# First norm's root applied at the evacuations, keys and values between the two query groups, HGRN sigmoids one panel later

## The reference

```python
def rmsnorm(x, g):
    y = x * lax.rsqrt(jnp.mean(x * x, axis=-1, keepdims=True) + EPS)
    return y * g

u = rmsnorm(h, norm_mix_g)
p = jnp.einsum('bsd,de->bse', u, w_in) + b_in
aq, ak, av, hq, hf, hi, hg, gate_a, gate_b = split_columns(p)
y_attn = sliding_window_sink_attention(aq, ak, av, attn_sinks)
y_hgrn = hgrn2_branch(hq, hf, hi, hg, lb, hgrn_norm_g)
#   in hgrn2_branch:
#   log_f = log(lb + (1 - lb) * sigmoid(hf));  k = (1 - lb) * sigmoid(-hf);  q = silu(hq)
```

## Time and profile before

| | us |
|---|---|
| median of 3 runs | 791.05 (790.82 to 792.37) |
| the profiled execution | 790.83 |
| its span | 789.1 |

### The profile page before, as it was taken

How to read it: one execution, slowest core, us unless ns; L and a number is a source line. 1 busy time by engine, 2 the same in 40 slices (tenths; PEclk the granted TensorE clock), 3 DMA queues, 4 the chain that set the end, 5 groups by cost and what they waited for, 6 DMA issues and landing times. The chain is left out here.

```text
span 789.1 us, 12516 instructions
## 1 busy us (share of the span) xinstructions
PE 777.0 (98%) x5048; PEld 687.0 (87%) x5048; DVE 607.1 (77%) x815; ACT 476.1 (60%) x727; POOL 18.6 (2%) x38
## 2 busy tenths in 40 slices
PE   8999999999999999999999999999999999999996
PEld 8978978898888898888888888999789999999885
DVE  5587788687887667887869897997878788777464
ACT  6855887568644384444334267876858667665451
POOL 3000002000200000000000000001000000000000
PEclk9999999999999999999999999999999999999999
DMA  8873644656546638799879993644363756555611
GB/s 302 296 261 127 227 138 149 208 186 215 174 161 213 214 107 283 269 305 315 276 242 339 336 380 126 222 135 133 108 213 111 237 175 200 167 172 170 240 53 54
DMA packets 106537, 162.54 MB, mean 206 GB/s; under 512 B 4576, under 2 KB 51824, under 8 KB 106480
## 3 DMA queue, kind: packets, MB, share of 16 engines
q1 hardware_dynamic: 106336, 161.48, 61.3%
q10 hardware_dynamic: 144, 0.26, 0.1%
HBM read 160.67 MB, written 1.06 MB: 205 GB/s over the span
## 5 line engine op out<-in xcount | busy, mean ns | idle before, releaser
L1175 DVE TENSOR_TENSOR wL<-raw,wH 128x2048 fp32r<-128x2048 f32 (+2 forms) x142 | 285.2, 2013 | 84.3 <-ACT wH L764 81.9
L764 ACT ACTIVATE wH<-raw 128x2048 fp32r<-128x2048 f32 (+1 forms) x114 | 212.1, 1864 | 91.7 <-PE ps L1866 61.1
L1863 PE MATMUL ps<-p1H,wH 128*128 128x256 f32 x784 | 224.0, 286 | 1.6 <-DVE arena L1175 0.8
L1863 PE MATMUL ps<-p1H,wL 128*128 128x256 f32 x784 | 221.2, 283 | 0.0
L1863 PE MATMUL ps<-p1L,wH 128*128 128x256 f32 x784 | 219.8, 283 | 0.0
L1863 PEld LDWEIGHTS ps<-p1H,wH 128*128 128x128 f32 x784 | 150.2, 192 | 5.5 <-DVE wL L1175 2.2
L1863 PEld LDWEIGHTS ps<-p1H,wL 128*128 128x128 f32 x784 | 150.2, 192 | 0.0
L1863 PEld LDWEIGHTS ps<-p1L,wH 128*128 128x128 f32 x784 | 149.5, 192 | 0.0
L1866 PE MATMUL ps<-wH,p1H 128*128 128x512 f32 x316 | 125.2, 396 | 0.0
L1866 PE MATMUL ps<-wL,p1H 128*128 128x512 f32 x316 | 123.2, 390 | 0.0
L1866 PE MATMUL ps<-wH,p1L 128*128 128x512 f32 x316 | 123.1, 390 | 0.0
(11 more groups left out here) (303 smaller groups left out, 946.3 us busy)
## 6 DMA issues: line engine op xcount, KB each, us to landing
raw<-in_w_in SPq DMA_DIRECT2D x37, 1024.0 KB, 6.1
raw<-in_w_ada SPq DMA_DIRECT2D x24, 1024.0 KB, 5.2
raw<-in_w_up SPq DMA_DIRECT2D x44, 512.0 KB, 4.7
raw<-in_w_ffn_gate SPq DMA_DIRECT2D x22, 512.0 KB, 4.3
raw<-in_w_ffn_up SPq DMA_DIRECT2D x22, 512.0 KB, 5.5
raw<-in_w_ffn_down SPq DMA_DIRECT2D x10, 1024.0 KB, 5.5
raw<-in_w_down SPq DMA_DIRECT2D x10, 1024.0 KB, 5.1
raw<-in_w_out SPq DMA_DIRECT2D x8, 1024.0 KB, 5.1
```

The source lines that it names most:

```text
L764: nc.scalar.activation(wH[:, q % NHL, 0:nk, 0:wd], raw[:, i % NRAW, 0:nk, 0:wd], ACT.Copy).then_inc(on.w_hi, 1)
L1175: return v.tensor_tensor(o, a, b, op)
L1863: last = mm(ps[:, t[1], 0:T], wt[:, slot, k, t[2]:t[2] + P], at_[:, k0 + k, :], start=st, stop=en)
```

## The change

Four things are altered, all in the first block.

- **Root.** The first norm no longer multiplies by 1/rms. x comes in four channel quarters (256 KB each, all tokens), each followed by one row block of the first weight panel. TensorE transposes one quarter (`turn_input`) ahead of the products and one behind each of the first three steps; ScalarE writes `p1H` straight from PSUM with the gain as scale, VectorE `p1L`. Squares and roots (`root_0`) follow behind the first panel, the spread behind the first tile of kv. 1/rms is multiplied in where products are evacuated: VectorE evacuates q, kv, hq, hf (`ROOTED`) with `rbs0`, and ScalarE then adds the bias in place; the token-major groups take it as a scalar of each token. `rbs0` lies in the memory of `dtW`, so `dtW` is filled in the first FFN.
- **Order.** q0, kv, q1; q0's evacuation stands behind kv's first panel event, `vectors` there too, `setup` behind q1's first panel. V is turned into bank 7, and the first `pt` waits for its copy.
- **Sigmoids.** Those of hq and hf move from the evacuation to the tail, behind the next group's first panel event.
- **Banks.** Some groups use other PSUM banks.

The diff, cut to its core:

```diff
+    for _name, _c, _b, _f in (("q", 0, 0, 2), ("hq", 1280, 0, 2), ("hf", 2304, 4 * _i, 2 - 2 * _i)):
+        GROUPS[f"{_name}{_i}"] = group("w_in", [(_c + _i * W, W)], cm_tiles(_b, _f), "DDDD", "P1")
+    for _name, _c, _b in (("hi", 3328, 2 - 2 * _i), ("hg", 4352, 2 * _i), ("ga", 5376, 2 - 2 * _i), ("gb", 6400, 2 - 2 * _i)):
...
+GROUPS["kv"] = group("w_in", [(1024, 256)], [("cm", 4, 0), ("cm", 5, P)], "DD", "P1")
...
+ROOTED = ["kv"] + [f"{_n}{_i}" for _i in range(2) for _n in ("q", "hq", "hf")]
...
-                tl.append(("evac", name))
-                if name.rstrip("0123456789") in ("f", "u", "xs", "bc", "hf"):
+                (later if name == "q0" else tl).append(("evac", name))
+                if name.rstrip("0123456789") in ("f", "u", "xs", "bc", "hq", "hf"):
                     later.append(("tail", name))
...
-    gemm("q0")
-    gemm("q1", [("vectors",)], [("setup",)])
+    gemm("q0", [("root",)])
+    gemm("kv", [("vectors",)])
     first = X(0, "ga0", 0)
-    gemm("kv", [], first[:-1] + [("v_turn",)] + first[-1:])
+    gemm("q1", [("setup",)], first[:-1] + [("v_turn",)] + first[-1:])
...
-    gemm("hi1", [("hdm", 1), ("hprep", 1, 0)], [("hprep", 1, 1)])
+    gemm("hi1", [("hdm", 1)], [("hprep", 1, 0), ("hprep", 1, 1)])
...
+            x = IN["x"][0].rearrange("(j p) n -> p j n", p=P)
             for k in range(KP):
+                sp.dma_start(res[:, :, wide(k)], x[:, :, wide(k)]).then_inc(on.in_x[k], 16)
                 sp.dma_start(raw[:, 0, k, :], first[:, k, 0:W]).then_inc(on.in_w0[k], 16)
                 if k == 0:
+                    sp.dma_start(par[:, 0:KD], IN["params"][:, 0:KD]).then_inc(on.in_g, 16)
+            sp.dma_start(par[:, KD:], IN["params"][:, KD:]).then_inc(on.in_par, 16)
```

ScalarE: the start, then the evacuation of q and the tail of hf:

```diff
+            def enter():
+
+                table(ACT.Sqrt)
+                act.wait_ge(on.in_g, 16)
+                for k in range(KD):
+                    if k % 2 == 0:
+                        act.wait_ge(on.ut_psum, k // 2 + 1)
+                    nc.scalar.activation(p1H[:, k], xT(k), ACT.Copy, scale=gain(0, k)).then_inc(on.uh_done, 1)
+                    if k < 4:
+                        first_hi(0, k, 1)
+                    elif k in (4, 5):
+                        first_hi(1, 2 * k - 8, 2)
+
+            def root_0():
+
+                for j in range(TB):
+                    square_x(j)
+                    root(0, j)
...
+                    if i == 0:
+                        act.wait_ge(on.in_par, 16)
+                        act.wait_ge(on.rb_psum, 1)
+                        nc.scalar.activation(rbs0, rb, ACT.Copy).then_inc(on.rb_copy, 1)
+                    for m in range(4):
+                        act.wait_ge(*EV[name, m])
+                        nc.scalar.activation(aQ[:, 4 * i + m], aQ[:, 4 * i + m], ACT.Identity,
+                                             bias=pc("b_in", 4 * i + m)).then_inc(on.evac_act, 1)
...
+                elif g == "hf":
+                    for m in range(4):
+                        act.wait_ge(*EV[name, m])
+                        nc.scalar.activation(T2[:, m], T1[:, m], ACT.Sigmoid, scale=-1.0,
+                                             bias=negb[:, 4 * i + m:4 * i + m + 1])
+                        nc.scalar.activation(T1[:, m], T1[:, m], ACT.Sigmoid,
+                                             bias=pc("b_in", 18 + 4 * i + m)).then_inc(on.evac_act, 1)
```

VectorE's evacuations:

```diff
+                if name in ROOTED:
...
+                    if name == "q0":
+                        dve.wait_ge(on.in_par, 16)
+                        dve.wait_ge(on.rb_copy, 1)
...
+                    for m, t in enumerate(GROUPS[name]["tiles"]):
+                        dve.wait_ge(on.tile_done, TILE[name, m])
+                        tt(to[m], ps[:, t[1], 0:T], rbs0, ALU.mult).then_inc(on.evac_dve, 1)
...
-                        tt(to, ps[:, GROUPS[name]["tiles"][j][1], :], rows(name)[0], ALU.add).then_inc(on.evac_dve, 1)
+                        stt(to, ps[:, GROUPS[name]["tiles"][j][1], :], R1[:, j:j + 1], rows(name)[0], ALU.mult,
+                            ALU.add).then_inc(on.evac_dve, 1)
```

TensorE:

```diff
+            def turn_input(c):
+
+                pe.wait_ge(on.in_x[c], 16)
+                if c > 1:
+                    pe.wait_ge(on.u_ready, 2 * c - 2)
+                for k in (2 * c, 2 * c + 1):
+                    for j in range(TB):
+                        last = tr(xT(k)[:, j * P:(j + 1) * P], res[:, j, k * P:(k + 1) * P])
+                last.then_inc(on.ut_psum, 1)
...
+                        if q == 0 and k < 3:
+                            turn_input(k + 1)
...
+                        if (name, part, m) == ("kv", 0, 0):
+                            spread_roots(0)
...
+                    if n == 0:
+                        warm(2)
+                        turn_input(0)
+                        warm(4)
+                        continue
```

and in `pt` of group 0:

```diff
+                    else:
+                        pe.wait_ge(on.v_done, 1)
```

More of the change, by code:

```diff
@@ L790, in square_x @@
             def square_x(j):
-                act.wait_ge(on.in_x[j], 16)
+                for c in range(4):
+                    act.wait_ge(on.in_x[c], 16)
                 if j:
@@ L1049, in _ @@
                     norm(e[1])
+                elif k == "root":
+                    root_0()
                 elif k == "evac":
@@ L1249, in read_ada, with enter @@
                    f(pc("b_ada", c, 16)), ALU.add).then_inc(on.ada_done, 1)
+            def enter():
+                dve.wait_ge(on.in_g, 16)
+                for k in range(KD):
+                    if k < 4:
+                        first_lo(0, k, 1, k == 3)
+                    elif k in (4, 6):
+                        first_lo(1, k - 4, 2, k == 6)
+                    dve.wait_ge(on.uh_done, k + 1)
+                    stt(p1L[:, k], xT(k), gain(0, k), p1H[:, k].bitcast(F32), ALU.mult, ALU.subtract).then_inc(on.u_ready, 1)
             def norm(n):
                 if n == 0:
-                    turn_over(n, 0)
+                    enter()
+                    return
                 if n == 4:
@@ L1474, in tail @@
                     tt(zL[:, 2 * i:2 * i + 2], zps if i in TOKENS_FIRST else ZT, zH[:, 2 * i:2 * i + 2].bitcast(F32), ALU.subtract).then_inc(on.z_ready, 1)
+                    if i == 5:
+                        dve.wait_ge(on.in_dtw, 16)
+                        step(v.memset(dtW[:], 0.0))
+                        v.tensor_copy(dtW[:, :, 0:8], dtw).then_inc(on.dtw_lo, 1)
                 elif g == "u":
@@ L1789, in late_turn, with spread_roots @@
             def late_turn(n, k):
[L1791 removed]
+                pe.wait_ge(*((on.rb_copy, n + 1) if k == 6 else (on.tmp_done, 8 * (n - 1) + 2)))
                 turn(n, (k,), range(TB)).then_inc(on.ut_psum, 1)
+            def turn_input(c):
[6 more added lines that the diff above has]
+                last.then_inc(on.ut_psum, 1)
+            def spread_roots(n):
+                for j in range(TB):
+                    pe.wait_ge(on.rd_done, 2 * n + j + 1)
+                    last = spread(rb[:, j * P:(j + 1) * P], R1[:, j:j + 1])
+                last.then_inc(on.rb_psum, 1)
             def gate_sum(g, i):
@@ L1894, in panel @@
                         early = k == 0 and name in NORM_OF
-                        if early:
+                        if q == 0 and k == 0:
+                            pe.wait_ge(on.uh_done, 1)
+                            pe.wait_ge(on.first_hi, 1)
+                            for t in g["tiles"]:
+                                product(t, 0, only=(0,))
+                        elif early:
                             pe.wait_ge(on.uh_done, 8 * NORM_OF[name] + 1)
@@ L1907, in panel @@
                                 pe.wait_ge(on.gate_done, 2 if name == "f0" else 4)
-                            last = product(t, k, only=(0, 2) if early else (0, 1, 2))
+                            last = product(t, k, only=(2,) if early and q == 0 else (0, 2) if early else (0, 1, 2))
                         if early:
```

184 lines of the change are left out of this document (72 added, 112 removed).

## The result

The changed kernel takes 803.3 us in the median of four runs (801.88 to 803.79), the kernel before 790.93 in four runs on the same chip: a ratio of 1.0150 (95% interval 1.0138 to 1.0163), slower by 12.4 us. The forecast was 801.1, the range 795.2 to 803.9. The profiled execution took 801.88 and its span is 800.1, 11.0 us more than the 789.1 of before. The other three took 803.2 to 803.8; an execution of that kind was profiled later (last experiment).

The account below looks back on a forecast made before the run. TensorE was taken to set the time once it has work, so a later stall adds in full. The profiled 790.83 plus 6.6 and 3.7 gave 801.1 us, range 795.2 to 803.9.

Parts of the forecast that it names:

- First term: From the start to group 0's first transposes of probabilities: late q1 part 1 and the waits after it, +6.6 us, start included.
- The wait of 2.2 us for bank 2: At ga0's first product: TensorE waits 2.2 us until VectorE evacuates q1's first tile, which holds the bank.
- The start: At the first panel: first product at 6.7 rather than 9.42, worth 1.6 us at the end of q0.
- The stall of 0.4 for quarter 1: In q0's first part, ahead of step 2: preparing quarter 1 takes 2.2 us against 1.9 of TensorE work, stall 0.4.
- Second term: At the tail of hf0: its late sigmoids delay PT and the transposes of group 5, +3.7 us (2.4 to 4.8).
- The line between the two rows of weights: Landing of q1 part 0's weights, read between panel 3 (21.54) and panel 4 (26.17): 24.5; 22.5 was taken.
- The step that ends at 14.7: At the start: the last of q0's four product steps, forecast to end at 8.6, 10.5, 12.8 and 14.7.
- rival 6: At every table switch on ScalarE: a drain is paid besides the load, 806.6 us in all, chance 0.02.
- Edits at nothing: Other evacuations, hf1's sigmoids, dtW's fill and queue changes: costed at nothing, bounds together -0.3 and +0.7.
- Rival 1: At the first group and hf0's tail: both stalls hidden, the start kept, 789.2 us, chance 0.07.

Follow-up runs that it names:

- last experiment: The changed kernel itself, unaltered, profiled a third time to see one of its slower executions: 803.78 us.
- the order at the front: Changed kernel with VectorE evacuating q0 and kv before the next low part, biases added later, vectors and setup behind q1 part 0: 795.26 us, ratio 1.0054.
- the early evacuation alone: Kernel with hf0 early, with the vectors put back behind q0 while VectorE still evacuates q0 and kv early: 794.89 us.
- the kernel with hf0 early: Changed kernel with the order at the front, V turned earlier, hf0's sigmoids back in its evacuation, and VectorE evacuating hf0 before a low part: 790.61 us, ratio 0.9996.

## Why the prediction was right, and where it was not

**First term, predicted +6.6, measured +7.1** (transposes of group 4 at 114.66 against 107.59). The chain came as written: weights at 22.8 (22.5), evacuation of q0 from 27.0, vectors to 33.7 (33.3), high part, low part, start at 37.98 (37.5), stall 4.45 (4.45); V's copy at the end of that chain let TensorE go at 55.07 (54.65). The runs show the mechanism from three sides: taken away by the order at the front, lengthened by the vectors done twice, halved by the early evacuation alone. Behind the stall two errors cancelled. The wait of 2.2 us for bank 2 wasn't there, since q1 part 1 took 8.1 us rather than 5.9 at the lower clock; with TensorE kept busy, the wait appears as 2.14, and in the third profile, where the panel took 1.5 us more, as 0.65. VectorE's chain, which the prediction had right, set ga0's start each time. That the clock cost no more than this wait could take up was luck: nothing in the prediction bounded it.

**The start, predicted 1.6 at the end of q0, measured 1.2** (20.9 against 22.1), and not steady: q0 part 1 began anywhere from 14.78 to 16.36 in the profiles of kernels with the same start, where 16.3 was the row of before. In the changed kernel it doesn't matter: the chain runs from the landing of q1 part 0's weights. The first product came at 5.87, before the 6.7 of the prediction, for the second lot of warming began at 4.42 rather than 4.9 and took 1.45 us up to the first product rather than 1.8; with eight matmuls at the lower clock throughout it took 1.57 (4.46 to 6.03 in the kernel with hf0 early), so the clock had little part in it. The stall of 0.4 for quarter 1, ahead of step 2, wasn't there. Instead 1.00 us stood ahead of step 1, since the second weight row had not landed until 7.4, and 0.39 ahead of part 1. The step that failed is that I asked of no later weight row when it lands.

**Second term, predicted +3.7, measured +4.0** in the profiled execution (11.08 at the panel behind the transposes of group 5, less 7.07). Gaps 1.23 (1.05) and 2.03 + 0.28 (2.7); from start to start they cost 0.5 us more than their idle time. Eight sigmoids took 3.3 us (3.1), at 0.40 each.

**Slips in the prediction's working.** The line between the two rows of weights gives 24.7 us and not 24.5; 22.8 was measured, near the 22.5 taken. The step that ends at 14.7 holds a second wait of 0.4 us that is not named. In rival 6 the two terms should be 10.7 and 5.1 and not 10.3 and 5.5, with the same sum. None of them enters the forecast, since the chain starts from the 22.5 taken.

**What was missed: the clock behind a stall.** Where the clock falls behind the gap at group 5, the second term is 5.6 rather than 4.0; that is about what lies between the profiled 801.88 and the median of 803.3. The other 0.8, from 801.1 to 801.88, are the two terms (0.5 and 0.3). The prediction held a stall to cost its own length. The Trainium skill ("TensorE: Matmul & The Clock Gate", HAM oscillation — how this bites in real kernels) says that the lower clock comes back after an idle gap and that the work behind it pays. The trace agrees, with 0.51 for 5.2 us, and I had not priced it. Here a gap of 2 us cost 3.6 where no other wait took it up (vectors put back behind q0: 2.05 and 1.5).

**Edits at nothing, -0.3 to +0.7.** In the changed kernel nothing of them shows. But that was cover: with the sigmoids back in place hf0's two-step evacuation cost 1.1 to 1.2 us at TensorE, until it was made early. Rival 1, both stalls hidden, I had at 789.2; with both mended and hf0 early the kernel stands at 790.6. The start gives less than its 1.6, and 0.60 us at the first transposes is left. No version that was tried is measurably faster than the kernel before.

**Rival 6**, a drain of 1.4 us at each switch of tables: the Trainium skill ("ScalarE: Activation LUTs", What ACT_TABLE_LOAD costs) states it. Six loads in a row at 1.28 with 0.22 between them, and a stall that grew by 4.51 us for three more, rule it out here.

## What to carry to other kernels

When one evacuation is split over two in-order queues, ask of the first step what stands ahead of it there: each time VectorE's product stood behind a weight's low part, ScalarE stood still and everything queued on it came later. Count the stall behind the stall (here a bank) before hoping for a gain from moving one wait: with the vectors moved 4.4 us went and 5.4 came. And a stall of TensorE is to be priced with the slower clock that may follow, 1.5 to 2.5 us behind the stalls of 2.0 to 9.0 us here, unless another wait takes that up.

## What the runs showed of the hardware that I had not expected

- Behind 4.45 us without work TensorE ran 5.2 us at a granted clock of 0.51, behind 8.96 us for 5.4 us at 0.50: twice the idle time, nearly the same price (2.3 and 2.5 us on a panel of 5.8). The price varies with the same program and stall, though: 1.5 us in the third profile, behind 3.97 us.
- Behind 2.0 us it fell in some executions and not in others of the same kernel; where it did, there and in other kernels, it cost 1.5 to 1.6 us.
- A TensorE stall can be filled with products that nobody reads, which held the clock at 1.00 through it, and the clock fell later, at the next wait, all the same.
